# Head norms of tokens-first q and k in three small steps, units two slots apart; the gains moved into the rotary tables and ScalarE's copy; reciprocal roots in 9 steps for 12

## What is computed

```python
def first_block(...):
    h = rms_norm(x, g_mix)
    q, k, v, z, xbc, dt_raw = split(h @ w_in)                    # 16 heads of 64; q, k, v have 1024 columns each
    attn = dilated_attention(q, k, v, positions, g_q, g_k)       # rms_norm of q and k by head (gains g_q, g_k of 64),
                                                                 # rotary turn of the first 16 of each head's 64,
                                                                 # softmax with a mask, times v
    ssm = ssd_mixer(z, xbc, dt_raw, ...)                         # state-space branch, with four group norms
    x = x + concat(rms_norm(attn), ssm) @ w_out
    x = x + cross_attention(rms_norm(x), rms_norm(mem), ...)
    x = x + square(relu(rms_norm(x) @ w_up)) @ w_down
```

## Time and profile before

| | |
|---|---|
| median of 3 runs | 2676.41 us (2674.36 to 2676.97) |
| the profiled execution's own time | 2671.09 us |
| its span, first to last instruction | 2669.3 us |
| TensorE busy | 2630.5 us (99%) |
| VectorE busy | 1772.6 us (66%) |
| ScalarE busy | 1337.3 us (50%) |
| GpSimd busy | 110.7 us (4%) |
| mean granted TensorE clock | 0.992 |
| bytes read | 482.87 MB, 182 GB/s over the span |

### The profile page before, as it was taken

The page is one execution under the profiler, slowest core; times in us unless marked ns, Lnnn a source line. Parts: engine busy times, 40 slices in busy tenths (PEclk is TensorE's granted clock), DMA queues, the critical chain, the costliest instruction groups (busy, mean ns, idle before and its releaser), DMA issues.

```text
span 2669.3 us, 51932 instructions
## 1 busy us (share of the span) xinstructions
PE 2630.5 (99%) x22010; PEld 2566.2 (96%) x22010; DVE 1772.6 (66%) x2667; ACT 1337.3 (50%) x1817; POOL 110.7 (4%) x76
## 2 busy tenths in 40 slices
PE   9999899999999999999999999999999999999998
PEld 9987799899999999999899999999999999999997
DVE  7787779675555555565787786556776656665666
ACT  6474566454344443444445774444455435543553
POOL 2000021010000000000000000000300000000003
PEclk9999999999999999999999999999999999999998
DMA  7544446465555655555454556565465555565552
GB/s 257 176 142 140 163 164 197 143 206 196 192 196 192 196 192 196 191 196 184 158 174 151 174 176 197 196 191 189 148 200 194 193 196 192 196 193 196 192 193 98
DMA packets 137176, 488.34 MB, mean 183 GB/s; under 512 B 15472, under 2 KB 18160, under 8 KB 136944
## 3 DMA queue, kind: packets, MB, share of 16 engines
q1 hardware_dynamic: 136656, 484.76, 55.0%
q10 hardware_dynamic: 288, 0.26, 0.0%
HBM read 482.87 MB, written 2.10 MB: 182 GB/s over the span
## 4 chain that ended last, share of the span: by engine, by line
PE 92%; DVE 6%; ACT 1%; issue 0%; DMA 0%; SPq 0%; POOL 0%; ACTq 0%; DVEq 0%
PE ps L835 91%; DVE WL L1879 2%; PE ps L838 1%; DVE XL L1887 1%; DVE T L1887 1%; DVE xT L1879 1%; ACT WH L1311 0%; DVE small L1887 0%; DMA raw<-in_w_in 0%; DVE T L1879 0%; DVE XL L1879 0%; ACT xT L1311 0%; DVE small L1879 0%; ACT P L1311 0%; DVE small L2136 0%
## 5 line engine op out<-in xcount | busy, mean ns | idle before, releaser
L1879 DVE TENSOR_TENSOR WL<-raw,WH 128x1024 fp32r<-128x1024 f32 (+1 forms) x910 | 1124.7, 1240 | 762.2 <-ACT WH L1311 761.8
L1311 ACT ACTIVATE WH<-raw 128x1024 fp32r<-128x1024 f32 (+1 forms) x910 | 961.6, 1058 | 1260.4 <-PE ps L835 1257.0
L835 PE MATMUL ps<-XH,WH 128*128 128x256 f32 x4768 | 1326.6, 278 | 7.1 <-DVE WL L1879 4.5
L835 PE MATMUL ps<-XL,WH 128*128 128x256 f32 x4768 | 1317.7, 276 | 0.0
L835 PE MATMUL ps<-XH,WL 128*128 128x256 f32 x4768 | 1317.6, 276 | 0.0
L835 PEld LDWEIGHTS ps<-XH,WH 128*128 128x128 f32 x4768 | 893.7, 187 | 12.7 <-issue 11.6
L835 PEld LDWEIGHTS ps<-XL,WH 128*128 128x128 f32 x4768 | 893.7, 187 | 1.8 <-issue 1.0
L835 PEld LDWEIGHTS ps<-XH,WL 128*128 128x128 f32 x4768 | 893.7, 187 | 0.3
L835 PE MATMUL ps<-AH,WH 128*128 128x256 f32 x1856 | 513.0, 276 | 0.6 <-DVE AL L1879 0.4
L835 PE MATMUL ps<-AL,WH 128*128 128x256 f32 x1856 | 512.3, 276 | 0.0
L835 PE MATMUL ps<-AH,WL 128*128 128x256 f32 x1856 | 512.3, 276 | 0.0
(11 more groups left out here) (228 smaller groups left out, 1635.4 us busy)
## 6 DMA issues: line engine op xcount, KB each, us to landing
raw<-in_w_up SPq DMA_DIRECT2D x304, 512.0 KB, 4.0
raw<-in_w_in SPq DMA_DIRECT2D x223, 512.0 KB, 3.5
raw<-in_w_down SPq DMA_DIRECT2D x216, 512.0 KB, 3.5
raw<-in_w_out SPq DMA_DIRECT2D x64, 512.0 KB, 3.5
raw<-in_w_gates SPq DMA_DIRECT2D x64, 512.0 KB, 4.3
raw<-in_w_ckv SPq DMA_DIRECT2D x16, 512.0 KB, 3.5
raw<-in_w_cq SPq DMA_DIRECT2D x8, 512.0 KB, 3.9
raw<-in_w_co SPq DMA_DIRECT2D x8, 512.0 KB, 3.2
```

Source lines behind the costliest of these rows:

```text
L835: return e.matmul(out, l, r, start=start, stop=True, skip_group_check=True)
L1311: return e.activation(out, x, func, **kw)
L1879: return e.tensor_tensor(out, a, b, op)
```

## The change

1. **qk_rs is split.** `qk_sum` takes the sums by head in a slot of its own, `qk_rs` the root in the next. A unit now has six steps in six slots (`qk_sq`, `qk_sum`, `qk_rs`, `qk_gain`, `qk_tr`, `qk_copy`).
2. **The second unit of a chunk starts two slots after the first** instead of one. The last `qk_copy` of a chunk moves two slots later, and with it the softmax of all heads, what is made of their output (`ma_hi`, `ma_lo`) and the two row norms behind it (`norm_rs` of norms 1 and 2 from slot 112 to 114).
3. **rcol leaves the head norm.** ScalarE squares the raw q or k; the eps that is added ahead of the root is eps divided by rcol squared (`least`, one instruction in the first `norm_rs`), so the root comes out with rcol in it. `qk_rs` loses its last instruction, and `qk_sq` no longer reads rcol.
4. **Gains.** The gains of the 16 turned columns are multiplied into the tables of cosines and sines once (`wave`, step `rope_gain` in slot 49, four instructions of 128x32); the gains of the other 48 are the `scale` of ScalarE's `qk_copy`, per partition, since there the features are on the partitions. The eight `scalar_tensor_tensor` of `qk_gain` become one `tensor_tensor` of 128x512 with the head's root broadcast.
5. **Roots.** The integer guess is one instruction, and one Newton step plus one step of higher order stand in place of three Newton steps: with the scaling 9 instructions that wait for one another for 12. For roots of 2 columns, squares and products are one `scalar_tensor_tensor` a column, two side by side: 10 instructions in a chain of 7 stages.

```diff
-        t = E("qkqk"[j // 2], j // 4) + 1 + j % 2
-        rope.append(P.chain(t, j, ("qk_sq", "qk_rs", "qk_gain", "qk_tr", "qk_copy"),
+        t = E("qkqk"[j // 2], j // 4) + 1 + 2 * (j % 2)
+        rope.append(P.chain(t, j, ("qk_sq", "qk_sum", "qk_rs", "qk_gain", "qk_tr", "qk_copy"),
...
-                on.wait_ge(*s("norm_rs", 1))
...
-                fn(T("qk", j)[:, :], x[:, :], ACT.Square, scale=rcol[:, t:t + 1]).then_inc(s["qk_sq"], 1)
+                fn(T("qk", j)[:, :], x[:, :], ACT.Square).then_inc(s["qk_sq"], 1)
...
+                half = stat[:, 22:24] if cols else v
+                on.wait_ge(*own.now)
+                if cols:
+                    ts(half, v, -0.5 * RATE, None, ALU.mult)
+                ts(out.bitcast(I32), v.bitcast(I32), -0.5, 1597463007.0, ALU.mult, ALU.add).then_inc(*own.up())
+                on.wait_ge(*own.now)
+                square_by(half, -0.5 * RATE)
+                stt(out, q, 1.5 * RATE, out, ALU.add, ALU.mult).then_inc(*own.up())
+                on.wait_ge(*own.now)
+                square_by(v, 1.0)
+                stt(q, q, -1.25 / RATE ** 3, q, ALU.add, ALU.mult).then_inc(*own.up())
+                on.wait_ge(*own.now)
+                return stt(out, q, 1.875 / RATE, out, ALU.add, ALU.mult)
...
-                rsqrt(r[:, 0:8], r[:, 8:16], 8, 1.0 / 64, EPS).then_inc(*own.up())
-                on.wait_ge(*own.now)
-                ts(r[:, 0:8], r[:, 0:8], rcol[:, t:t + 1], None, ALU.mult).then_inc(s["qk_rs"], 1)
+                rsqrt(r[:, 0:8], r[:, 8:16], 8, 1.0 / 64, least[:, t:t + 1]).then_inc(s["qk_rs"], 1)
...
-                for h in range(8):
-                    m = stt(y[:, 64 * h:64 * h + 64], x[:, 64 * h:64 * h + 64], r[:, h:h + 1], g, ALU.mult, ALU.mult)
+                tt(y, x[:, :].rearrange("p (h d) -> p h d", d=64), r[:, 0:8].unsqueeze(2).to_broadcast([128, 8, 64]),
+                   ALU.mult).then_inc(*own.up())
```

More of the change, by code:

```diff
@@ L26 @@
 MASKED = -3.0e38
+RATE = 0.375 ** 0.2
 NP = 4
@@ L1434, in qk_copy @@
                 on.wait_ge(*s("qk_tr", j + 1))
-                fn(out, S("qk", j)[:, :].rearrange("p (f t) -> p f t", f=4), ACT.Copy).then_inc(s["qk_copy"], 1)
+                fn(out, S("qk", j)[:, :].rearrange("p (f t) -> p f t", f=4), ACT.Copy,
+                   scale=V(("g_qrest", "g_krest")[j // 2 % 2])).then_inc(s["qk_copy"], 1)
             def v_copy(u):
@@ L1925, in root_of, with square_by @@
             def root_of(out, v, q):
+                n = v.shape[1]
+                cols = [slice(c, c + 1) for c in range(n)] if n == 2 else []
+                def square_by(x, rate):
+                    for c in cols:
+                        m = stt(q[:, c], out[:, c], out[:, c], x[:, c], ALU.mult, ALU.mult)
+                    if not cols:
+                        tt(q, out, out, ALU.mult).then_inc(*own.up())
+                        on.wait_ge(*own.now)
+                        m = stt(q, q, rate, x, ALU.mult, ALU.mult)
+                    m.then_inc(*own.up())
+                    on.wait_ge(*own.now)
+                half = stat[:, 22:24] if cols else v
                 on.wait_ge(*own.now)
-                ts(q.bitcast(I32), v.bitcast(I32), 1, None, ALU.logical_shift_right).then_inc(*own.up())
+                if cols:
+                    ts(half, v, -0.5 * RATE, None, ALU.mult)
+                ts(out.bitcast(I32), v.bitcast(I32), -0.5, 1597463007.0, ALU.mult, ALU.add).then_inc(*own.up())
                 on.wait_ge(*own.now)
-                ts(out.bitcast(I32), q.bitcast(I32), -1.0, 1597463007.0, ALU.mult, ALU.add).then_inc(*own.up())
-                for i in range(3):
-                    on.wait_ge(*own.now)
[L1933 to L1940, removed]
+                square_by(half, -0.5 * RATE)
[5 more added lines that the diff above has]
+                return stt(out, q, 1.875 / RATE, out, ALU.add, ALU.mult)
             def later_taps(src, dst, taps):
@@ L2131, in rope_cos, with rope_gain @@
                 reduced(cosA[:, :], 0.25).then_inc(s["rope_cos"], 1)
-            def qk_rs(j):
-                r, t = root(5 + j % 4), qk_of(j)[2]
+            def rope_gain(_):
+                on.wait_ge(*s("rope_sin_act", 1))
+                on.wait_ge(*s("rope_cos_act", 1))
+                for i, name in enumerate(("g_q", "g_k")):
+                    for n, angle in enumerate((cosA, sinA)):
+                        m = tt(wave[:, i, n, :].rearrange("p (t d) -> p t d", t=2),
+                               angle[:, :].rearrange("p (t d) -> p t d", t=2),
+                               V(name, 0, 16).unsqueeze(1).to_broadcast([128, 2, 16]), ALU.mult)
+                m.then_inc(s["rope_gain"], 1)
@@ L2152, in qk_gain @@
[L2152 to L2153 removed]
+                on.wait_ge(*s("rope_gain", 1))
                 by_cos, by_sin = (turn[:, n, :].rearrange("p (h d) -> p h d", d=16) for n in range(2))
[L2155 to L2156 removed]
+                for n, by in enumerate((by_cos, by_sin)):
+                    row = wave[:, j // 2 % 2, n, 16 * t:16 * t + 16].unsqueeze(1).to_broadcast([128, 8, 16])
@@ L2677, in vector @@
                     qk_rs(u)
+                for u in P("qk_sum", t):
+                    qk_sum(u)
+                for u in P("rope_gain", t):
+                    rope_gain(u)
                 for u in P("rope_cos", t):
```

34 lines of the change are left out of this document (20 added, 14 removed).

## The result

| | before | after |
|---|---|---|
| median | 2676.3 us (2674.36 to 2676.97, 4 runs) | 2650.77 us (2650.35 to 2651.01, 4 runs) |
| ratio, with its 95% interval | | 0.9906 (0.9888 to 0.9923) |
| the profiled execution's own time | 2671.09 us | 2651.01 us |
| its span | 2669.3 us | 2649.2 us |

The change makes the kernel 0.94% faster, 25.5 us by the medians. The profiled execution, on which the sum was made, was foreseen at 2650.4 us with a span of 2648.6; it came out at 2651.01 and 2649.2. So the sum held to 0.6 us, and what failed was the way from the profiled execution to the median.

What follows compares the result with a forecast made beforehand. TensorE was taken as the bound: its matmuls, waits and half clock. Waits 16.2 plus clock 6.0 less new waits 1.5 gave 20.7 us off the 2676.4 us median, so 2655.7 us, range 2652 to 2662.

Steps and rivals of the forecast that it cites:

- the five waits: TensorE waiting for VectorE between 190 and 330 us: two at `ssd_y`, three at `qk_tr`, 16.24 us together.
- The waits: Slots 58 to 95: 16.24 us become about 1.5, as new waits of 0.8 (slot 60) and 0.7 us (slot 61).
- The unit's price: One head-norm unit on VectorE: sum 0.7, root 1.8, `qk_gain` 1.5 us; from 5.86 to 4.0 us.
- Waits 3, 4, 5: Slots 65 to 71, 81 to 87 and 89 to 95: all three waits go, the fourth with 0.7 us to spare.
- Slots 97 to 125: Softmax, `ma_lo` and row norms come two slots later; no change in time taken.
- The clock term: Behind waits of 2.92, 3.15 and 4.67 us, TensorE works 12.9 us at half clock; 6.0 us is regained.
- The sum: 16.2 + 6.0 - 1.5 = 20.7 us less; the profiled execution's 2671.09 us becomes 2650.4.
- Short waits that bring half clock: Rival: the new short waits in slots 60 and 61 bring a slow stretch; 2657.5 to 2660 us, 15%.
- The old wait that comes back: Rival: an old wait stays or returns in slots 112 to 125, or broadcast costs 1.65 us; 2658 to 2661 us, 10%.
- The roots that buy more: Rival: pairs overlap or `ssm_rs` is under 1.9 us, so new waits fall below 0.5; 2654 us, no chance given.
- The slower case: Rival: TensorE waits for banks where softmax shares slots 84 to 90; 6 us slower, 2683 us, 3%.
- the case without effect: Rival: the waits hang on a buffer or transfer, not VectorE's load; 2676 us, 4%.

Runs made afterwards that it cites:

- the kernel with the waits put back: The changed kernel with four more sums by head in slots 58 and 60, bringing back waits at the two `ssd_y`: 2658.32 us.
- the old roots: The changed kernel with roots of 12 instructions in place of 9: 2653.56 us.
- the eight products: The changed kernel with the products by the head's root as eight instructions of 64 columns instead of one broadcast product: 2652.27 us.
- the halves of this change: The kernel before with only the sum split and units two slots apart: 2654.54 us; the changed kernel with the units' old place, smaller work kept: 2653.77 us.
- the filler: 17 and 16 extra matmuls, results thrown away, in the two waits put back into the changed kernel by four more sums by head: 2654.94 us.

## Why the prediction was wrong, point by point

- **What bounds the kernel**: right. The time went where the five waits and the half clock were.
- **The waits**: 16.24 us were to become 1.5. They became 0.57 + 0.32 = 0.9, at the two places foreseen. The first was to be 0.8: VectorE's mask was done at 200.14 as foreseen (200.1), and TensorE came 0.3 us later than written. The second was to be 0.7: `ssm_rs` took 1.71 instead of 1.9, and TensorE was later here too.
- **The unit's price**: 0.7, 1.8, 1.5 foreseen; 0.71, 1.75, 1.54 measured. The broadcast along the inner axis costs nothing: 0.69 us, the lower of the two bounds.
- **Waits 3, 4, 5**: gone as written; with no wait at `sm_tr` or `qk_tr` either.
- **Slots 97 to 125**: "I take no change" is right for the waits, 0.17 for 0.18, and the softmax's matmuls moved two slots and cost the same. For TensorE's own work it is wrong: the matmuls of `w_out_s` cost 1.8 us more. The prediction has no term for it.
- **The clock term**: 6.0 us foreseen for 12.9 us at half clock, which is 0.46 for each. That is what the rows of the matmuls show, 0.427 for 0.23 us. In slots 57 to 66 TensorE's busy time fell by 3.65 us where 8.3 us of work had been at half clock, 0.44; in the kernel with the waits put back it is 3.0 us more (33.7 for 30.7) for 6.8, 0.44. Over all six steps busy time fell by 6.4 us outside `w_out_s`. So the term holds for the profiled execution.
- **The sum**: 20.7 foreseen, 20.1 measured between the profiled executions. Waits 0.6 better, busy time outside `w_out_s` 0.4 better, `w_out_s` 1.8 worse. That the sum held to 0.6 us is in part luck, as these errors have opposite signs.
- **The step that failed** is the last: "The median of the runs is 5.3 us above that execution, twice the spread of the runs; I know no cause and carry it over". The 5.3 us were mostly half clock behind the same waits that the sum had just taken away. The text had the pieces: that a wait costs a slow stretch in some cases and not in others, and that the profiled execution had been spared behind the 3.46 us. In the other two profiles of before TensorE is busy 4.2 and 4.1 us longer over the four stretches with waits (111.5 and 111.4 us for 107.3), so to the changed kernel it falls by 8.8 and 8.7 us instead of 4.6; with their 16.7 and 15.4 us of waiting over that of the changed kernel, that is 25.5 and 24.1 us. These two executions took 2678.01 and 2674.85 us, one above and one below the median of 2676.3, and the medians are 25.5 us apart. The range failed with it: its low end took the 5.3 us as fixed, where the case that they go too gives 2650.4.
- **The rivals.** Short waits that bring half clock: not in this kernel, where waits of 0.57 and 0.32 us stand 4.6 us apart and the clock stays 1.00; but 1.44 us did it with the old roots and 1.51 us did not with the eight products, so the rival was nearer than its 15%. The rule of short idles between groups of matmuls (the Trainium skill, page TensorE: Matmul & The Clock Gate, section "A second HAM failure mode: psum-queue depth-cycling") gave 2659 and is not borne out at this length of wait. The old wait that comes back: no, the broadcast product costs 0.69 us and the wait behind slot 125 is 0.17. The roots that buy more: `ssm_rs` was shorter than 1.9, as it has it, but the first new wait stayed above its 0.5. The slower case and the case without effect: no sign of either.

## What to carry to other kernels

Where the median of a kernel lies above its profiled execution by more than the runs spread, the difference is a cost with a place: look for the waits behind which the clock could have fallen and did not, and count that loss into what their removal is worth. A long wait of TensorE costs itself and a draw for half clock, at 0.46 us for each us of work done at it; if the wait can't go, matmuls with thrown-away results in it kept the clock up here (5.6 us). Two cures for the same wait don't add: the halves of this change gave 84% and 87% of it alone. And a sum that comes out right is not yet a sum whose terms are right: compare the busy time stage by stage, as here for `w_out_s`, before a difference is put down to the clock.

## What the runs showed of the hardware that was not expected

- The same program's time ranges over 7.8 us (2670.94 to 2678.74). In the three profiles the largest part of the difference is whether the clock falls behind the same waits (4.2 of 6.9 us, and 4.1 with a span 3.8 us longer). 3.46 us was followed by full clock once and by half clock twice, 1.44 us by half, 1.51, 1.66 and 2.33 us by full.
- A matmul of 512 columns takes 0.23 us at full clock and 0.427 at half, start to start, so half clock loses 0.46 us a us and not 0.5.
- The same 384 matmuls at full clock take 46.5 us in the changed kernel and 44.7 before, in every profile of each. The cause is open.
- Half clock between two waits for VectorE costs nothing, because the second wait is shorter by as much: 2.12 us, against 3.85 us from the start of the filler to `ssd_y` with full clock, and the two `ssd_y` are 0.3 us apart. In these kernels only the half clock behind the last wait was paid for.
- A product of 128x512 float32 out of PSUM with an operand broadcast along the inner axis takes 0.69 us, as much as with a full table.
